# One-hots of the gate build laid out by pairs of tokens, and the last small projection behind the second expert layer

## The reference, cut to what matters

```python
def peer_ffn(x, ...):                      # 16384 experts = 128 x 128 keys
    q = (x @ w_peer_q).reshape(B, S, 8, 2, 128)
    s = einsum('bshcd,hcnd->bshcn', q, peer_subkeys)
    # the best 16 of 128 keys on both sides, the best 16 of the 256 pairs
    experts = i1 * N_KEYS + i2             # 8 heads x 16 = 128 experts per token
    gates = softmax(best_s)
    act = gelu(einsum('tkd,td->tk', peer_u[experts], x))
    return einsum('tk,tkd->td', gates * act, peer_v[experts])

h = h + peer_ffn(rms_norm(h, ffn_norm), ...)
gate = sigmoid(rms_norm(h, ple_norm) @ w_ple_gate)      # "pg" in the kernel
h = h + gate * (p @ w_ple_proj)                         # "pp" in the kernel, p: 256 features
return rms_norm(h, final_norm)
```

## Time and profile before

| | |
|---|---|
| median of 3 runs | 3992.37 us (3987.19 to 3993.74) |
| profiled execution, its own time | 4002.21 us |
| its span in the trace | 4000.4 us |
| mean granted clock of PE | 0.979 |
| busy PE / DVE / ACT / POOL | 95% / 52% / 39% / 62% |
| chain that ended last | PE 75%, POOL 11%, DVE 8%, issue 3% |
| of it, line 498 / 1002 / 951 | 47% / 18% / 3% |

### The profile page before, as it was taken

One profiled execution on the slowest core, in us unless ns is written; L12 is line 12 of the kernel. 1 busy time (PEld: TensorE's weight loads), 2 busy tenths in 40 slices (PEclk: granted clock), 3 DMA queues, 4 the chain that ended last, 5 costly groups with the idle time before them and its releaser, 6 DMA issues.

```text
span 4000.4 us, 72623 instructions
## 1 busy us (share of the span) xinstructions
PE 3812.0 (95%) x30508; PEld 3694.4 (92%) x30508; DVE 2066.2 (52%) x2905; ACT 1562.4 (39%) x1966; POOL 2470.0 (62%) x970
## 2 busy tenths in 40 slices
PE   6999998899999889999999999999999999999998
PEld 3799898899998879999999999999999999999988
DVE  6776257773425464462025695654444555534445
ACT  5313433333334334454444344224443333344443
POOL 0157975687886638698888795018885000178876
PEclk9999999999999999999999999999999999999999
DMA  8466752464743425355555454335554444445543
GB/s 328 175 251 242 273 201 106 178 232 148 265 178 118 151 77 208 139 178 181 185 183 189 175 183 174 124 127 187 188 186 163 161 154 163 153 174 182 187 147 127
DMA packets 98268, 714.37 MB, mean 179 GB/s; under 512 B 11024, under 2 KB 11152, under 8 KB 12048
## 3 DMA queue, kind: packets, MB, share of 16 engines
q1 hardware_dynamic: 97056, 703.65, 48.5%
q10 hardware_dynamic: 1008, 7.79, 0.5%
HBM read 709.30 MB, written 2.10 MB: 178 GB/s over the span
## 4 chain that ended last, share of the span: by engine, by line
PE 75%; POOL 11%; DVE 8%; issue 3%; ACT 2%; DMA 1%; DVEq 0%; POOLq 0%; SPq 0%; ACTq 0%
PE bank L498 47%; PE bank L1002 18%; POOL unit_lo L456 11%; PE bank L951 3%; PE bank L627 1%; DVE unit_lo L1644 1%; DMA ring<-in_w 1%; PE bank L527 1%; PE bank L566 1%; ACT unit_hi L1024 1%; PE bank L510 0%; PE bank L736 0%; PE bank L903 0%; ACT att_s L1238 0%; DVE c_raw L2011 0%
## 5 line engine op out<-in xcount | busy, mean ns | idle before, releaser
L456 POOL TENSOR_TENSOR unit_lo<-ring,unit_hi 128x1024 fp32r<-128x1024 f32 x956 | 2445.2, 2574 | 1415.6 <-ACT unit_hi L1024 1413.6
L1024 ACT ACTIVATE unit_hi<-ring 128x1024 fp32r<-128x1024 f32 x1204 | 1239.5, 1055 | 1255.0 <-PE bank L498 548.0
L498 PE MATMUL bank<-xl_hi,unit_hi 128*128 128x256 f32 x4976 | 1418.3, 285 | 48.8 <-POOL unit_lo L456 27.8
L498 PE MATMUL bank<-xl_hi,unit_lo 128*128 128x256 f32 x4976 | 1400.9, 282 | 0.0
L498 PE MATMUL bank<-xl_lo,unit_hi 128*128 128x256 f32 x4976 | 1400.4, 281 | 0.0
L498 PEld LDWEIGHTS bank<-xl_hi,unit_hi 128*128 128x128 f32 x4976 | 947.6, 190 | 60.5 <-POOL unit_lo L456 26.5
L498 PEld LDWEIGHTS bank<-xl_lo,unit_hi 128*128 128x128 f32 x4976 | 946.9, 190 | 0.5
L498 PEld LDWEIGHTS bank<-xl_hi,unit_lo 128*128 128x128 f32 x4976 | 947.0, 190 | 0.0
L1002 PE MATMUL bank<-w_r,unit_hi 128*128 128x256 f32 x4096 | 726.4, 280 | 6.1 <-DVE w_r L2410 6.1
L1002 PEld LDWEIGHTS bank<-w_r,unit_hi 128*128 128x128 f32 x4096 | 627.4, 188 | 6.5 <-issue 6.5
L1002 PE MATMUL bank<-w_r,unit_lo 128*128 128x256 f32 x2048 | 572.5, 280 | 0.0
(11 more groups left out here) (421 smaller groups left out, 5031.3 us busy)
## 6 DMA issues: line engine op xcount, KB each, us to landing
ring<-in_w SPq DMA_DIRECT2D x669, 1024.0 KB, 4.8
resid<-in_xT ACTq DMA_DIRECT2D x1, 2048.0 KB, 15.7
tmp_ctx<-in_ctxT ACTq DMA_DIRECT2D x1, 2048.0 KB, 11.9
rnn_gates<-in_rgw ACTq DMA_DIRECT2D x1, 2048.0 KB, 9.1
out<-resid SPq DMA_DIRECT2D x4, 512.0 KB, 2.6
con<-in_con ACTq DMA_DIRECT2D x1, 512.0 KB, 3.4
con<-in_con ACTq DMA_DIRECT2D x1, 448.0 KB, 7.4
p_tmp<-in_pT ACTq DMA_DIRECT2D x1, 256.0 KB, 3.5
```

What stands on the lines that cost most here:

```text
L456: pool.tensor_tensor(lb[b][:], ring[slot][:, f * HALF:(f + 1) * HALF], hb[b][:].bitcast(F32), ALU.subtract).then_inc(lo_done, 1)
L498: mm = pe.matmul(bank[(s.t0 + tile[m]) % TILES][:, 0:T], w[b][:, (i % 8) * P:(i % 8 + 1) * P], mv[x][:, k, :], start=(k == 0 and w is hb a ...
L1024: act.activation(hb[b][:], ring[slot][:, f * HALF:(f + 1) * HALF], ACT.Copy).then_inc(hi_done, 1)
```

## The change

Three parts:

The one-hot tiles and `places` change their layout from [key, token] to [pair of tokens, key, 2], so that the two tokens of a pair are neighbours and the keys stand 4 bytes apart for one token instead of 16. `places` shrinks to [key, 2] and is read again for each pair. `ob` is written by two instructions, one for each part of the gate, and counted twice. PE reads the columns of a token from the new place; the number and shapes of its matmuls stay.

The stage pp moves behind peer_v of round two. It uses half banks 0 to 3 as eight tiles (`pp_tile`); PE starts it when the first two banks have been added to the residual; ACT, no longer DVE, copies its results to `pps`, two tiles at a time, between the norm's high parts and squares, which get an order written out by hand. POOL splits pp's units first, then two groups of the norm, then pg's first unit (before: one unit, then the groups).

pg waits for pp's first twelve tiles, and behind its first unit for the others.

```diff
     ("peer_u1", "NNNN", I2 // 4, 1, "A"),
-    ("pp", "NN", 1, 8, "D"),
     ("peer_v1", "NNNN", I2 // 4, 0, "D"),
+    ("pp", "NN", 1, 8, "A"),
     ("pg", "N" * 16, 1, 1, "D"),
...
+        def pp_tile(i):
+            return bank[i % 8 // 2][:, i % 2 * T:(i % 2 + 1) * T]
...
-        oa = [zone("hot1_0", 96, [P, NKEY, TG], F16), zone("hot1_1", 98, [P, NKEY, TG], F16)]
-        oe = [zone("hot2_0", 100, [P, I2, TG], F16), zone("hot2_1", 101, [P, I2, TG], F16)]
-        ob = [zone("hotg_0", 102, [P, 2, I2, TG], F16), zone("hotg_1", 104, [P, 2, I2, TG], F16)]
-        places = nc.alloc_sbuf_tensor_at("places", [P, NKEY, TG], F16, offset=z0 + 116 * KB)
+        oa = [zone("hot1_0", 96, [P, TG // 2, NKEY, 2], F16), zone("hot1_1", 98, [P, TG // 2, NKEY, 2], F16)]
+        oe = [zone("hot2_0", 100, [P, TG // 2, I2, 2], F16), zone("hot2_1", 101, [P, TG // 2, I2, 2], F16)]
+        ob = [zone("hotg_0", 102, [P, 2, TG // 2, I2, 2], F16), zone("hotg_1", 104, [P, 2, TG // 2, I2, 2], F16)]
+        places = nc.alloc_sbuf_tensor_at("places", [P, NKEY, 2], F16, offset=z0 + 116 * KB)
...
(POOL)
-                    if s.name in ("peer_v0", "pp"):
+                    if s.name == "pg":
+                        split_lo(s.name)
+                    if s.name in ("peer_v0", "peer_v1"):
                         pool.wait_ge(lo_done, 2 * s.n0)
...
(PE, build)
-                    pe.wait_ge(S("hot_g"), i + 1)
+                    pe.wait_ge(S("hot_g"), 2 * i + 2)
...
-                            mm = pe.matmul(bank[5 + k][:, t * I2:(t + 1) * I2], oa[k][:, :, t], ob[k][:, x, :, t],
+                            mm = pe.matmul(bank[5 + k][:, t * I2:(t + 1) * I2], oa[k][:, t // 2, :, t % 2], ob[k][:, x, t // 2, :, t % 2],
...
(PE, behind peer_v of round two)
+            s = PLAN["pp"]
+            pe.wait_ge(S("p_ready"), 1)
+            pe.wait_ge(S("rms_t"), NG + 1)
+            for j in range(2):
+                for f in range(2):
+                    b = (2 * (s.n0 + j) + f) % NBUF
+                    pe.wait_ge(lo_done, 2 * (s.n0 + j) + f + 1)
+                    if j == 0 and f == 1:
+                        pe.wait_ge(S("rms_t"), NG + 2)
+                    for t in range(4):
+                        i = 8 * j + 4 * f + t
+                        if j == 1 and i % 2 == 0:
+                            pe.wait_ge(tile_free["A"], TILES + s.ta + i - 6)
+                        for k in range(2):
+                            for w, x in ((hb, 0), (hb, 1), (lb, 0)):
+                                mm = pe.matmul(pp_tile(i), ...)
+                    mm.then_inc(half_done, 1)
+            pe.wait_ge(tile_free["A"], TILES + s.ta + 12)
...
(ACT, behind peer_v of round two; ahead(s, 0) makes pp's second unit, ahead(s, 1) pg's first)
+            def pp_out(q):
+                act.wait_ge(half_done, NBUF + 2 * s.n0 + q + 1)
+                for i in range(4 * q, 4 * q + 4, 2):
+                    act.activation(flat(pps[:, i:i + 2, :]), bank[i % 8 // 2][:], ACT.Copy
+                                   ).then_inc(tile_free["A"], 2)
+            ahead(s, 0, 0, True)
+            rest_hi(0)
+            rest_square(0)
+            pp_out(0)
+            rest_hi(1)
+            pp_out(1)
+            ahead(s, 1, 0, True)
+            rest_square(1)
+            rest_hi(2)
+            pp_out(2)
+            rest_hi(3)
+            pp_out(3)
+            rest_square(2)
+            rest_square(3)
...
(DVE, hot)
+                    def keys(n, k0):
+                        return places[:, k0:k0 + n, :].unsqueeze(1).to_broadcast([P, TG // 2, n, 2])
+
+                    def tokens(row, n):
+                        return row[:, i * TG:(i + 1) * TG].rearrange("p (g t) -> p g t", t=2).unsqueeze(2
+                                                                    ).to_broadcast([P, TG // 2, n, 2])
                     k = i % 2
-                    go(dve.tensor_tensor(oe[k][:], places[:, r * I2:(r + 1) * I2, :],
-                                         bc(picked[:, 1, i * TG:(i + 1) * TG], I2), ALU.is_equal))
+                    go(dve.tensor_tensor(oe[k][:], keys(I2, r * I2), tokens(picked[:, 1, :], I2), ALU.is_equal))
...
-                    dve.tensor_tensor(ob[k][:], oe[k][:].unsqueeze(1).to_broadcast([P, 2, I2, TG]),
-                                      gb[:, :, i * TG:(i + 1) * TG].unsqueeze(2).to_broadcast([P, 2, I2, TG]), ALU.mult
-                                      ).then_inc(S("hot_g"), 1)
+                    for x in range(2):
+                        dve.tensor_tensor(ob[k][:, x, :, :, :], oe[k][:], tokens(gb[:, x, :], I2), ALU.mult
+                                          ).then_inc(S("hot_g"), 1)
...
-                if r == 1:
-                    run("pp", lambda i, ps, _: dve.tensor_copy(at(pps, i), ps))
```

More of the change, by code:

```diff
@@ L448, in body @@
                         for j in range(s.npi):
-                            if j == 1 and isinstance(it, int) and it == 0:
+                            if j == 1 and isinstance(it, int) and it == 0 and s.name != "pg":
                                 split_lo(s.name)
@@ L979, in _ @@
                                 build(it * 2 + j // 2, j // 2)
-                    pe.wait_ge(S("p_ready"), 1)
-                    run("pp", [[pt_r[:, 0, :, :], pt_r[:, 1, :, :]]], per_tile=2)
                 s = PLAN[f"peer_v{r}"]
@@ L1008, in _, with pg_extra @@
                     body(it, False)
-            pe.wait_ge(S("rms_t"), NG + 2)
-            run("pg", [xc], extra=lambda it, j: ple_sums(3, NG) if j == 0 else None)
+            s = PLAN["pp"]
[13 more added lines that the diff above has]
+                            for w, x in ((hb, 0), (hb, 1), (lb, 0)):
+                                mm = pe.matmul(pp_tile(i),
+                                               w[b][:, (2 * t + k) * P:(2 * t + k + 1) * P], pt_r[:, x, k, :],
+                                               start=(k == 0 and w is hb and x == 0), stop=(k == 1 and w is lb),
+                                               skip_group_check=True)
+                    mm.then_inc(half_done, 1)
+            pe.wait_ge(tile_free["A"], TILES + s.ta + 12)
+            def pg_extra(it, j):
+                if j == 0:
+                    ple_sums(3, NG)
+                    pe.wait_ge(tile_free["A"], TILES + PLAN["pg"].ta)
+            run("pg", [xc], extra=pg_extra, early=True)
             acc_sum(bank[7][:, 0:T], 5, "rms_sum")
@@ L1380, in _ @@
                         u_beside(it, j)
-                if r == 1:
-                    run("pp")
                 s = PLAN[f"peer_v{r}"]
@@ L1396, in _, with rest_hi @@
             act.wait_ge(S("wr_ready"), 2 * I2)
-            for g in range(NG):
+            s = PLAN["pp"]
+            def rest_hi(g):
                 act.wait_ge(S("rms_t"), NG + g + 1)
@@ L1400, in _, with rest_square @@
                                ).then_inc(S("n2_hi"), 1)
+            def rest_square(g):
                 act.activation(flat(rq3[:, g * GR:(g + 1) * GR, :]), flat(h[:, g * GR:(g + 1) * GR, :]), ACT.Square
                                ).then_inc(S("rms_in"), 1)
+            def pp_out(q):
[17 more added lines that the diff above has]
+            rest_square(3)
             s = PLAN["pg"]
@@ L2335, in _ @@
             go(dve.tensor_copy(picked[:], gT[:, 0:2, :]))
-            go(dve.tensor_copy(places[:], C("iota").unsqueeze(2).to_broadcast([P, NKEY, TG])))
+            go(dve.tensor_copy(places[:], C("iota").unsqueeze(2).to_broadcast([P, NKEY, 2])))
             event("gate_parts")
@@ L2342, in hot @@
                 def hot(i, r=r):
+                    def keys(n, k0):
[3 more added lines that the diff above has]
+                                                                    ).to_broadcast([P, TG // 2, n, 2])
                     k = i % 2
-                    go(dve.tensor_tensor(oe[k][:], places[:, r * I2:(r + 1) * I2, :],
-                                         bc(picked[:, 1, i * TG:(i + 1) * TG], I2), ALU.is_equal))
+                    go(dve.tensor_tensor(oe[k][:], keys(I2, r * I2), tokens(picked[:, 1, :], I2), ALU.is_equal))
                     dve.wait_ge(S("g_done"), r * GROUPS + 1 + i)
-                    dve.tensor_tensor(oa[k][:], places[:], bc(picked[:, 0, i * TG:(i + 1) * TG], NKEY), ALU.is_equal
+                    dve.tensor_tensor(oa[k][:], keys(NKEY, 0), tokens(picked[:, 0, :], NKEY), ALU.is_equal
                                       ).then_inc(S("hot_1"), 1)
                     sync()
-                    dve.tensor_tensor(ob[k][:], oe[k][:].unsqueeze(1).to_broadcast([P, 2, I2, TG]),
-                                      gb[:, :, i * TG:(i + 1) * TG].unsqueeze(2).to_broadcast([P, 2, I2, TG]), ALU.mult
-                                      ).then_inc(S("hot_g"), 1)
+                    for x in range(2):
+                        dve.tensor_tensor(ob[k][:, x, :, :, :], oe[k][:], tokens(gb[:, x, :], I2), ALU.mult
```

(2 more changed lines are left out.)

## The result

The changed kernel takes **3887.58 us**, the median of 4 runs (3869.74 to 3892.54); the kernel before took 3993.05 beside it (4 runs). The ratio is 0.9724, with a 95% interval of 0.9685 to 0.9763. The profiled executions are 4002.21 and 3889.79 us, 112.4 apart, where the sum said 78.

The account below looks back on a forecast made before the run. PE, busy 95% of the span and never pausing in the builds, was taken as the bound. The terms -59.4 - 5 - 17.2 - 2.6 + 6 = -78 us took the profiled 4002.2 to 3924, or 3914 as median; range 3884 to 3950.

Parts of the forecast that it names:

- the sum: Whole kernel: -59.4 - 5 - 17.2 - 2.6 + 6 = -78 us.
- Nearest row: the load of the weights: Gate builds on PE: the load's columns set the matmul spacing, 61 ns instead of 119, saving 59.4 us over 64 builds.
- The other bound: Gate builds on PE: if only the moving columns count, at 0.46 ns each, 64 take 30 ns.
- Rival two: Gate builds on PE: everything packs, spacing 30 to 50 ns; at 40 ns another 21 us, 3893; chance 0.16.
- The clock, -5: Behind four of six double builds: half clock for 3.4 us disappears as double builds shorten to 2.0 us; 5 us back.
- DVE, hidden at nothing: Gate builds on DVE: one more instruction, at most +0.15 us per build, hidden by DVE's waits, so costed at nothing.
- Rival four: Gate builds: DVE pays per row of two and bounds round one's builds; at +6 us per build 4094; chance 0.03.
- rival three: Gate builds: DVE leaves packed mode at rows of two elements, +1.5 us per build, 3927 us; chance 0.07.
- The pause, -17.2 and -2.6: Between peer_u1 and peer_v1: without pp 19.5 us becomes 2.3, -17.2; the slow clock behind it goes too, -2.6.
- The tail, +6: Behind peer_v1: pp's new place costs +4.5 us by steps, about +10 if the clock stays low; +6 taken.
- Rival one: Gate builds on PE: the weight load is the bound, saving at most 10 us for all, 3968 us; chance 0.09.
- five: Whole change: build spacing stays 119 ns and pp only swaps one pause for another, 3982 us; chance 0.03.

Follow-up runs that it names:

- the four-times kernel: The changed kernel with the matmuls of each build issued four times over (64 for 16, same result): execution 3983.64 us.

## Why the prediction was wrong, and where it was right

**The step that failed: "Nearest row: the load of the weights ... With a few ns for the handover ... I take 61."** Measured: 30 ns. The 57 ns for the load's columns came from the difference between a load of 4 columns (84) and one of 128 columns that is f32. For fp16 at a 4-byte step the load lasts 97, so that by the same subtraction its columns take 13 ns, not 57. And even the 16-byte load allows a spacing of 62, so the earlier trace rows with its 146 beside a spacing of 119 said nothing of the load. The other bound, from the moving columns of the packed matmuls (0.46 ns a column, 30 ns), was the value. Rival two had it, with a chance of 0.16, a spacing of 30 to 50 ns, and 3893 us for 40 ns. The miss of the profiled executions, 112.4 against 78, is 30.8 us from this term, 1.8 from the clock and 3.1 from the tail and the kernel's end, less 1.5 that passed ahead of the first build.

**The clock, -5.** Measured -5.7 in round one's build stretch. (The other 1.1 of the ledger stand at the start of peer_u1, where no step looked.) The forecast that the clock stands behind the new double builds came true; its reason, that they are short, is not the one that counts, for the four-times kernel shows that the shortness was not needed. A better-fed array of the old length keeps the clock too.

**DVE, hidden at nothing.** Right: the instructions last 414 to 417 and 683 ns, and PE waits for none in either build stretch. The cut instruction costs 2 x 0.417, as priced. The prediction's reserve (22.0 us of DVE against PE's 27.5) shrank further than it thought, as PE was quicker: per four units PE now needs 4 x 5.66 + 5 x 0.49 = 25.1. Rival four did not come; rival three's mechanism came at rows of one element.

**The pause, -17.2 and -2.6.** Measured -17.3 and -2.6. The rows of round one were a good model of the pause. The -2.6 was luck in part: the prediction has no slow clock behind a pause of 2.3 us, from one row. In the 16 traces there are 30 such pauses ahead of a peer_v, and behind 13 of them the clock is at 0.50 for 3.4 us, which costs 1.5 us (363.3 us for peer_v instead of 361.8); pp's move alone had it at this place.

**The tail, +6.** Measured +3.4. The working's steps gave 4.5 and their times hold: pp starts 4.9 us after peer_v (4.7), pg 18.6 after it (19.2), behind ACT, which costs PE 0.3 us. The rest, up to 6, was put on for a clock that might stay down through pp; it was down for 3.4 us.

**Rival one (the load is the bound, 3968) and five (3982)** are out: loads that last 97 ns follow each other at a spacing of 30.

**What no step asked:** every weight matmul was taken at 0.118 us, before and after. The runs show that there are two paces; that both kernels had the same one behind their builds is why the sum was not disturbed by it. That was luck, since the change did touch the builds, and another cut of them moved the pace.

## What to carry to other kernels

Count the bytes that a matmul's moving operand steps per column, not only its columns: for fp16 the time went with them beyond 4 bytes, and a full busy share, with or without a lower clock behind it, hides this. When a bound is taken from a row, take it from one of the same type, and ask which of two overlapped things the row measures; here the duration of a load that never was the limit stood for one that was. And compare matmuls per us of untouched stretches between two traces: a pace of 118 instead of 113 ns over long rows was worth more than the tail that two experiments were spent on.

## What the runs showed of the hardware

- The fp16 moving operand is read at 8 to 9 bytes of step per ns: about 1.8 ns a column at 16 bytes, 0.97 at 8 (with the load at 8 too), 0.46 at 4, and no less at 2. A load of 128 fp16 columns at 16 bytes allows a spacing of 62 ns, one at 4 bytes 25. How long a load lasts says less: at 16 bytes 170 ns beside packed moving columns and 146 beside wide ones, at 4 bytes 97 and 115.
- Pairs of load and matmul go at 30 ns with 64 columns and at 25 with 32, where half of 30 would be 15: something other than the columns sets the 25. The Trainium skill (TensorE: Matmul & The Clock Gate, "Back-to-back issue gap") gives about 81 ns for such pairs with 128 columns, a size that no run here has, and for matmuls without the load N/2.4 + 2.5 ns, not under some 25 ns up to 64 columns. The pairs here agree with the second: it makes 29.2 ns for 64 columns.
- The same 256-column f32 matmuls run at two paces at full clock, 113 and 118 ns; a row keeps the one in which it starts, and the short matmuls ahead of it can change it.
- A clock of 0.50 for 3.4 us came behind 13 of 30 pauses of 2.3 us, and also with no pause at all, behind double builds with a 16-byte step (3.6 to 3.8 us); it came behind none of the six double builds of 3.9 us whose matmuls go at 30 ns.
- DVE's fp16 instructions with a broadcast operand keep the packed mode in rows of two (1024 elements in 683 ns) and lose it with a single element innermost (1252).
- Four DVE multiplications of 256 f32 take 1.14 us alone, 3.1 when one POOL instruction crosses them, and 8.25 when POOL runs four in a row. The Trainium skill (SBUF — State Buffer, "Who interferes with whom") has the one of DVE, in a mode that uses both its ports, and POOL that issues first block the other for a whole instruction; the 3.1 and 8.25 us agree with that.
